# The last stage's sum of eight expert rows per token: TensorE takes all eight, VectorE none

## What is computed

```
y    = einsum('nef,efd->nd', silu(hg) * hu * gates[..., None], exp_w_down)   # 8 of 64 experts have a gate
y_sh = (silu(x @ sh_w_gate) * (x @ sh_w_up)) @ sh_w_down
x    = layer_norm(DN_ALPHA * x + gate2 * (y + y_sh), ln2_g, ln2_b)
```

## Time and profile before

| | |
|---|---|
| median of three runs | 2030.36 us (2021.64 to 2034.74) |
| profiled execution | 2021.33 us, span 2019.5 us |
| mean granted TensorE clock over the span | 0.956 |
| TensorE matmul busy | 1820.4 us, 90% of the span |
| TensorE weight load busy | 1308.7 us, 65% |
| VectorE busy | 1005.0 us, 50% |
| GpSimd busy | 694.4 us, 34% |
| ScalarE busy | 494.1 us, 24% |
| last stage | 1939.7 to 2019.5 us, the last two of the page's 40 slices of time |

### The profile page before, as it was taken

The page is one execution under the profiler, slowest core; times in us unless marked ns, Lnnn a source line. Parts: engine busy times, 40 slices in busy tenths (PEclk is TensorE's granted clock), DMA queues, the critical chain, the costliest instruction groups (busy, mean ns, idle before and its releaser), DMA issues. The chain is left out here.

```text
span 2019.5 us, 44508 instructions
## 1 busy us (share of the span) xinstructions
PE 1820.4 (90%) x17916; PEld 1308.7 (65%) x17916; DVE 1005.0 (50%) x2082; ACT 494.1 (24%) x936; POOL 694.4 (34%) x1036
## 2 busy tenths in 40 slices
PE   7989999989788999999998779997799999999966
PEld 2555655455656776777776569555678888778822
DVE  3768865728534555555654436456322222222238
ACT  2111132130133433444444122011112222212200
POOL 5518000000023434344443223231344444444435
PEclk9989999989899999999999889997899999999988
DMA  9143557673142321222210176400799989999865
GB/s 300 52 136 92 193 183 250 202 265 113 56 138 70 96 57 34 75 72 75 72 57 9 46 279 230 143 32 11 292 351 332 316 298 326 347 331 337 299 252 231
DMA packets 228319, 355.90 MB, mean 176 GB/s; under 512 B 38305, under 2 KB 156852, under 8 KB 224452
## 3 DMA queue, kind: packets, MB, share of 16 engines
q1 hardware_dynamic: 201358, 300.73, 43.8%
q0 software_dynamic: 24496, 45.01, 6.3%
q10 hardware_dynamic: 2310, 7.92, 1.1%
HBM read 307.11 MB, written 84.34 MB: 194 GB/s over the span
## 5 line engine op out<-in xcount | busy, mean ns | idle before, releaser
L2877 DVE TENSOR_TENSOR me_hh<-me_sg,ps_ju 128x128 f32<-128x128 f32 x76 | 21.8, 287 | 386.4 <-PE ps_jd L2829 374.6
L452 PE MATMUL ps_s<-hT,w_in_sb 128*128 128x512 f32 x432 | 194.6, 604 | 0.0
L2821 PE MATMUL ps_jg<-me_xT,me_wg 128*128 128x128 f32 x1216 | 149.1, 276 | 0.0
L1349 PE MATMUL ps_gs<-hT,gt_w 128*128 128x512 f32 x256 | 145.5, 651 | 3.2 <-PEq L76 3.2
L2821 PE MATMUL ps_ju<-me_xT,me_wu 128*128 128x128 f32 x1216 | 148.2, 275 | 0.0
L2829 PE MATMUL ps_jd<-me_wd,me_hh 128*128 128x512 f32 x304 | 143.1, 593 | 2.4 <-DVE me_yb L2883 2.4
L2821 PEld LDWEIGHTS ps_jg<-me_xT,me_wg 128*128 128x128 f32 x1216 | 142.9, 193 | 0.1
L452 PEld LDWEIGHTS ps_s<-hT,w_in_sb 128*128 128x128 f32 x432 | 81.7, 194 | 93.4 <-issue 92.7
L2821 PEld LDWEIGHTS ps_ju<-me_xT,me_wu 128*128 128x128 f32 x1216 | 141.9, 192 | 0.0
L2850 ACT ACTIVATE me_xT<-ps_jx 128x1024 f32<-128x1024 f32 x77 | 78.9, 1025 | 210.0 <-PE ps_jx L2812 207.7
L2812 PEld LDWEIGHTS ps_jx<-ident,me_xg 128*128 128x128 f32 x616 | 79.0, 192 | 69.7 <-DMA me_xg<-h_dram,me_ids 43.3
(11 more groups left out here) (574 smaller groups left out, 3838.8 us busy)
## 6 DMA issues: line engine op xcount, KB each, us to landing
me_wg<-in_exp_w_gate SPq DMA_DIRECT2D x76, 512.0 KB
me_wu<-in_exp_w_up SPq DMA_DIRECT2D x76, 512.0 KB
me_wd<-in_exp_w_down SPq DMA_DIRECT2D x76, 512.0 KB
w_ad_sb<-in_w_ada SPq DMA_DIRECT2D x32, 512.0 KB
w_in_sb<-in_w_in SPq DMA_DIRECT2D x31, 512.0 KB, 4.2
gt_w<-in_w_in SPq DMA_DIRECT2D x24, 512.0 KB, 4.6
cb_rows<-yj_dram SPq DMA_DIRECT2D x6, 2048.0 KB
zr<-in_w_ada SPq DMA_DIRECT2D x4, 2048.0 KB, 9.4
```

What stands on the lines that cost most here:

```text
L452: mm(ps_s[:, b, :], w_in[:, r, k, :], hT[:, k, 0:TS], start=(k == 0), stop=(k == KT - 1))
L1349: nc.tensor.matmul(ps_s[:], w[:, t % WR, k, :], hT[:, k, 0:TS], start=(k == 0), stop=(k == KT - 1))
L2821: last = mm(o[:, 0:P], w[:, s, k, :], xT[:, s % 2, k, :], start=(k == 0), stop=(k == KT - 1))
```

## The change

All eight rows of a token go to TensorE, so a tile is 16 matmuls in the program and one weight instruction on GpSimd writes eight diagonals. VectorE's two row instructions and the semaphore `e_used` are gone. `cb_diag` has two buffers, which tiles 0, 1 and 2 share (tile 2 takes that of tile 0). GpSimd therefore writes the weights in the order 0, 1, 3, 4, 2, and before those of tile 2 waits until TensorE has finished tile 0 (`e_mm` of 2). TensorE waits for all five weight instructions before tile 2, 3 or 4. The room behind the pieces in `h2T` and `mT` is filled exactly.

```diff
-        NR, HALF, BYPE = 8, TOPK // 2, 6
+        NR, HALF, BYPE = 8, TOPK // 2, TOPK
         own = sb("cb_rows", [P, NR - 3, HALF, D])
-        diag = sb("cb_diag", [P, 3, BYPE, P])
+        diag = sb("cb_diag", [P, 2, BYPE, P])
...
         def weight(t):
 
-            return diag[:, t] if t < 3 else late[t - 3]
+            return diag[:, t % 2] if t < 3 else late[t - 3]
...
                     if q >= NR:
                         t, h = (q - NR) // 2, q % 2
                         sp.wait_ge(m.e_mm, 2 * t + h + 1)
-                        if h:
-                            sp.wait_ge(m.e_used, (t + 1) * (TOPK - BYPE))
...
-                for t in range(NT):
+                for t in (0, 1, 3, 4, 2):
+                    if t == 2:
+                        pool.wait_ge(m.e_mm, 2)
                     weights(t)
...
             def _(pe):
                 for t in range(NT):
-                    pe.wait_ge(m.e_dg, t + 1)
+                    pe.wait_ge(m.e_dg, t + 1 if t < 2 else NT)
                     if t >= 2:
                         pe.wait_ge(m.e_sum, t - 1)
...
                 for t in range(NT):
                     x, c = m.acc[:, t], t // (NT - 1)
-                    for j in range(BYPE, TOPK):
-                        b, n = piece(t, j), t * (TOPK - BYPE) + j - BYPE
-                        dve.wait_ge(m.e_land[b % NR], 16 * (b // NR + 1))
-                        if j > BYPE:
-                            dve.wait_ge(m.e_used, n)
-                        V.scalar_tensor_tensor(x, rows[b % NR][:, j % HALF], m.gj[:, t, j:j + 1], x, ALU.mult, ALU.add).then_inc(m.e_used, 1)
-                    dve.wait_ge(m.e_used, (t + 1) * (TOPK - BYPE))
                     dve.wait_ge(m.e_mm, 2 * t + 2)
                     V.tensor_tensor(x, x, ps[:, t % 2], ALU.add).then_inc(m.e_sum, 1)
```

More of the change, by code:

```diff
@@ L2920, in combine_phase @@
         m.e_land = sems(nc, m, " ".join(f"e_land{r}" for r in range(NR)))
-        (m.e_used, m.e_dve, m.e_sqv, m.e_sq, m.e_nrm, m.e_pl, m.e_ln, m.e_out, m.e_dg, m.e_mm, m.e_sum, m.e_first, m.e_aff, m.e_outl) = sems(
-            nc, m, "e_used e_dve e_sqv e_sq e_nrm e_pl e_ln e_out e_dg e_mm e_sum e_first e_aff e_outl")
+        (m.e_dve, m.e_sqv, m.e_sq, m.e_nrm, m.e_pl, m.e_ln, m.e_out, m.e_dg, m.e_mm, m.e_sum, m.e_first, m.e_aff, m.e_outl) = sems(
+            nc, m, "e_dve e_sqv e_sq e_nrm e_pl e_ln e_out e_dg e_mm e_sum e_first e_aff e_outl")
         left, right = slice(0, D // 2), slice(D // 2, D)
         def weight(t):
-            return diag[:, t] if t < 3 else late[t - 3]
+            return diag[:, t % 2] if t < 3 else late[t - 3]
         def piece(t, j):
```

## The result

| | before | after |
|---|---|---|
| median of 20 runs | 2030.68 us (2021.64 to 2039.33) | 2042.83 us (2034.39 to 2052.52) |
| ratio | | 1.0053, 95% interval 1.0036 to 1.0069 |
| profiled execution: span | 2019.5 us | 2045.2 us |
| last stage, from SyncE's first load to the end of the span | 2019.5 - 1939.72 = 79.8 us | 2045.2 - 1954.97 = **90.2 us** |

The change makes the kernel slower by about 0.5%, or some 11 us. The forecast was 2040.4 us and +10.0 us. The two spans differ by 25.7 us, and 15.25 of these lie ahead of the last stage, in code that the change does not touch. In the ten profiled executions of this study the stage begins anywhere from 1939.72 to 1958.57. So the stage is compared by its own length, and the whole program only by the ratio.

A forecast was written before the change was run, and what follows sets the result against it. VectorE bounds now at 12.07 us a tile, with TensorE close behind and without gaps. TensorE's added records (+10.8 us) and the shorter tail (-0.77) give +10.0 us, 2040.4 us on the median, range 2030 to 2049.

The forecast's parts named there:

- TensorE's tile against VectorE's: Last stage: TensorE's tile grows from 10.3 to 13.72 us, more than VectorE's present 12.07, which decides the sign.
- TensorE, added: Last stage: eight more records a tile at 0.429 us; TensorE ends at 2015.67, the last sum comes 10.8 us later.
- Slow records at the start: Tile 0 on TensorE: five records at 1.2 GHz as before; with the skill's 14, 3.9 us more.
- Going by the row: Tile 0's slow records: taken as five from the profile row, instead of the Trainium skill's 6, 11 or 14.
- The tail: From last L3012 to the end: 13.78 us instead of 14.55, as L3014 finds GpSimd done, -0.77 us.
- Its wait ahead of each sum: VectorE before each L3012: waits 6.9 us for TensorE, so the gain of the removed rows stays there.
- 1.24 us in every tile: Expected sign in the profile after: L3014 takes 1.24 us in every tile, against 2.01 in the last tile before.
- That hold: Tile 0: weights meeting VectorE's L3014 hold one of them back by under 2 us, on no path.
- Weights, order, loads: GpSimd and SyncE: weight instructions of 1.95 us, tile 2's with 10 us of cover; later loads cost 0.
- a free L3014: Last tile: GpSimd's affine work ends 13.48 us after the previous L3012, the next starts at 13.72; L3014 finds GpSimd done.
- The slower rival: TensorE waits at tile 2 and falls to the lower clock: one tile costs 13.7 us more, +23.7 in all; chance 0.06.

The follow-up runs named there:

- the square of four kernels: Six or eight rows' matmuls on TensorE, with or without VectorE's two: before 79.8 us, after 90.2, rows left out 74.6, matmuls added 89.9 (last stage).
- the addition alone: Kernel before plus four matmuls per tile into a spare PSUM tile, VectorE's rows kept: stage 89.9 us, ratio 1.0054.
- the removal: Kernel before with VectorE's two row instructions per tile left out, TensorE's twelve matmuls kept: stage 74.6 us, ratio 0.9969.
- Two buffers alone: Kernel before with two weight buffers, the new weight order and waits, six rows still on TensorE: stage 79.8 us, ratio 1.0007.
- the seven-row kernel: Changed kernel with seven rows on TensorE and one on VectorE: stage 81.4 us, ratio 1.0004.
- the late-weights kernel: Changed kernel with eight more GpSimd weight instructions ahead of tile 2's, forcing TensorE to pause: stage 100.2 us, one run.

## Why the prediction was right

- **TensorE's tile against VectorE's.** 13.72 against 12.07 us decided the sign. Shown by the square of four kernels: the addition alone has the whole loss, and the removal on top of it changes nothing.
- **TensorE, added.** The sum had TensorE run from 1944.74 to 2015.67, 70.93 us; the chain has 71.56. The 0.6 us are the slow records at the start. At 0.429 us a record and 0.59 for the last, 160 records are 68.8 us at the full clock, so the low clock cost 2.8 us, between six and seven records, where the trace of before has 12.60 - 10.46 = 2.1 us, five. In the eight-row kernel with the affine work on VectorE it is 2.1 again, so these 0.6 us are not of the change.
- **Slow records at the start.** In all ten profiled executions the first tile is longer than at the full clock by 2.1 to 2.8 us, which is five to six and a half records. That their number changes from run to run agrees with the Trainium skill (TensorE: Matmul & The Clock Gate, "What's actually happening"); the fourteen that it counted in another kernel were not seen here. Going by the row was right.
- **The tail.** Forecast 13.78 us, measured 2045.2 - 2031.43 = 13.77. L3014's counterpart, L3007, takes 1.24 us in the last tile, as forecast.
- **VectorE.** Its wait ahead of each sum was forecast at 6.9 us; it is 6.41 ahead of tile 1, where L3007 of tile 0 had been held by the weights (1.77 us, so the sign "1.24 us in every tile" did not come true), and 6.95 ahead of the last. That hold was named and priced at nothing, and it cost nothing, since VectorE waits for TensorE behind it.
- **Weights, order, loads.** 1.90 us against 1.95. TensorE has no wait for weights or, past the first, for rows. Two buffers alone cost nothing (79.8 us, and TensorE without a gap at tile 2).
- **Stage.** Forecast 2029.54 - 1939.72 = 89.8 us, measured 90.2. The sum was right to 0.4 us. That it is not closer is mostly the 0.6 us of slow records, less 0.15 us by which the first rows landed earlier. Over the whole program the ratio gives +10.8 us (7 to 14), far wider than that.
- **Mis-sized without effect.** GpSimd's affine work was taken over from before with 6.6 us a tile. It is 1986.31 + 2.34 - 1983.89 = 4.76 us. The 3.33 and 3.22 us of the earlier trace rows held waits for VectorE's row instructions, which the change had removed. With it the forecast of a free L3014 had more room than it knew: by its own numbers GpSimd is done 13.72 + 1.26 - 13.48 = 1.5 us ahead of L3014, and in the trace L2968 of tile 1 ends at 1999.50 + 2.34 = 2001.84 and L3007 of tile 2 begins at 2005.21, 3.4 us later.
- **The slower rival.** Its mechanism is real, its price was not. A pause is followed by the lower clock, but the fall costs 2.3 us. To reach 1% (20.3 us) it would have needed a pause of 20.3 - 10.0 - 2.3 = 8.0 us. The price of a whole tile at the lower clock was set against a row (tile 0) that already said otherwise; 0.06 was generous.

## What to carry to other kernels

Where two engines feed each other tile by tile, write down each one's busy time per tile before moving work between them: the result is the larger of the two as long as the loads keep up, and an engine without gaps in the trace pays in full for what it is given. Before moving work off the bounding engine, look at whether its instructions are longer than the same ones elsewhere in the trace. Here the second row instruction took 3.19 us in four tiles, and the pair of them only 2.69 in the tile where GpSimd was idle. That pointed to GpSimd's work. Moving this work to VectorE itself, as two instructions in the place of three, shortened the stage by 5.6 us, about as much as leaving out both rows (5.2), and cost TensorE nothing.

## What the runs showed of the hardware

- VectorE and GpSimd hold each other up in both directions. A row instruction of VectorE takes 1.28 us with GpSimd idle (in the seven-row kernel) and 3.19 beside it. GpSimd's affine instruction takes 2.34 us with VectorE idle or waiting and 3.33 beside the row instructions. A weight instruction takes 1.90 us, and 2.76 in the late-weights kernel, where also a residual instruction of VectorE (1.22 alone) takes 2.80. The ends fit a hold for a whole instruction: after the change GpSimd's weights end at 1976.54 + 1.90 = 1978.44, and L3007, begun at 1977.75, ends at 1979.52, 1.08 us later, little under its 1.23 alone. The Trainium skill (SBUF — State Buffer, "SBUF: two separate sides") says that whichever starts first gets the pair for the whole instruction; these rows agree. The sum of the PSUM bank (L3012) beside GpSimd takes 1.22 us as always.
- A fall of TensorE's clock after a pause of 7.86 us costs 2.3 us, about the same as at the start of the stage after 16 us without a matmul (2.1 to 2.8). The gap of 0.81 us ahead of tile 1 in the kernel before left the clock at 1.00.
- The loads are the next limit. With 10.3 us of TensorE per tile, TensorE asks for piece 8 some 49.4 us after the first load. In two of the five such kernels it landed at 50.1 us and TensorE waited (74.6 us where 73.8 were expected); in these two GpSimd's stores come earlier and move 0.89 and 1.05 MB between 2 and 49 us after the first load, against 0.66 before. With the affine work on VectorE the stores go through SyncE's queue, behind the loads: the slowest lands 27.1 us after its issue, and TensorE reaches tile 4 at 1997.31 - 1947.96 = 49.35 us without a wait.
